# Two stage ends worked tile by tile, and three hand-placed steps moved, in a kernel of two transformer blocks

## What is computed

```python
# first block
h = rmsnorm(x, norm_mix_g); proj = h @ w_in           # pooling mixer and dilated attention on proj
x = x + concatenate([y_pool, y_attn]) @ w_out
h = rmsnorm(x, norm_mlp_g)
x = x + square(relu(h @ w_up)) @ w_down               # hidden width 8192
x = rmsnorm(x, norm_final_g)
# second block; the six mod vectors are silu(c) @ ada_w + ada_b
h = rms(x, norm_g[0]) * (1 + scale_m) + shift_m
proj = h @ w_in_2                                      # differential attention, mLSTM, GLA, S5
o_d = z * sigmoid(z @ s5_glu_w + s5_glu_b)             # z = gelu(S5 scan output), the fourth branch
merged = sum(sigmoid(h @ w_gate[i] + b_gate[i]) * (branch[i] @ w_branch[i]) for i in range(4))
x = x + gate_m * rms(merged @ w_out_2, norm_g[1])
h = rms(x, norm_g[2]) * (1 + scale_f) + shift_f
a, g = split(h @ ffn_w_in)                             # hidden width 5632
x = x + gate_f * rms((silu(a) * g) @ ffn_w_out, norm_g[3])
```

## Time and profile before

| | us |
|---|---|
| median of 3 runs (lowest, highest) | 2698.68 (2697.27, 2699.57) |
| the profiled execution | 2700.24 |
| its span in the profile | 2698.5 |
| PE busy in the span | 2636.2 (98%) |
| DVE busy | 1913.1 (71%) |
| ACT busy | 1251.6 (46%) |
| granted PE clock, mean | 0.995 |

### The profile page before, as it was taken

The page is one execution under the profiler, slowest core; times in us unless marked ns, Lnnn a source line. Parts: engine busy times, 40 slices in busy tenths (PEclk is TensorE's granted clock), DMA queues, the critical chain, the costliest instruction groups (busy, mean ns, idle before and its releaser), DMA issues.

```text
span 2698.5 us, 36266 instructions
## 1 busy us (share of the span) xinstructions
PE 2636.2 (98%) x13230; PEld 2216.3 (82%) x13230; DVE 1913.1 (71%) x2300; ACT 1251.6 (46%) x1515; POOL 280.9 (10%) x322
## 2 busy tenths in 40 slices
PE   8999999999999998999999999999999999999997
PEld 8898888888888886998977777788788888888886
DVE  6676677788778778765676888787755555555686
ACT  5445554444444445455455444444454444444443
POOL 0031041324132000061000000000000000000000
PEclk9999999999999999999999999999999999999999
DMA  9655777888788885856554665688556666666784
GB/s 338 209 162 196 235 261 251 281 275 266 250 282 274 272 271 172 278 165 216 165 164 156 229 217 185 205 306 293 197 184 191 190 191 190 191 188 193 263 292 154
DMA packets 289328, 607.03 MB, mean 225 GB/s; under 512 B 19472, under 2 KB 20688, under 8 KB 287296
## 3 DMA queue, kind: packets, MB, share of 16 engines
q1 hardware_dynamic: 284896, 579.41, 65.3%
q0 software_dynamic: 4320, 26.13, 2.6%
HBM read 594.17 MB, written 11.29 MB: 224 GB/s over the span
## 4 chain that ended last, share of the span: by engine, by line
PE 86%; DVE 6%; DMA 3%; ACT 3%; issue 2%; POOL 0%; SPq 0%; DVEq 0%; ACTq 0%; POOLq 0%
PE ps L577 84%; DVE w_lo L1845 2%; DMA w_raw<-in_w_in 2%; ACT w_hi L1224 1%; DVE arena L1840 1%; PE ps L682 1%; DMA w_raw<-in_w_up 1%; PE ps L709 0%; DMA w_raw<-in_w_gate 0%; DVE x L1855 0%; ACT arena L1482 0%; DMA w_raw<-in_w_down 0%; DVE arena L2174 0%; PE ps L693 0%; PE ps L672 0%
## 5 line engine op out<-in xcount | busy, mean ns | idle before, releaser
L1224 ACT ACTIVATE w_hi<-w_raw 128x1024 fp32r<-128x1024 f32 x900 | 950.6, 1058 | 1356.2 <-PE ps L577 1265.8
L1845 DVE TENSOR_TENSOR w_lo<-w_raw,w_hi 128x1024 fp32r<-128x1024 f32 x812 | 1016.0, 1254 | 653.5 <-ACT w_hi L1224 650.3
L577 PE MATMUL ps<-w_hi,hop_hi_part 128*128 128x512 f32 x2144 | 846.9, 395 | 12.2 <-DVE w_lo L1845 3.1
L577 PE MATMUL ps<-w_hi,hop_lo_part 128*128 128x512 f32 x2144 | 836.7, 390 | 0.0
L577 PE MATMUL ps<-w_lo,hop_hi_part 128*128 128x512 f32 x2144 | 836.3, 390 | 0.0
L577 PEld LDWEIGHTS ps<-w_hi,hop_hi_part 128*128 128x128 f32 x2144 | 403.6, 188 | 109.5 <-issue 15.6
L577 PEld LDWEIGHTS ps<-w_hi,hop_lo_part 128*128 128x128 f32 x2144 | 403.5, 188 | 85.2
L577 PEld LDWEIGHTS ps<-w_lo,hop_hi_part 128*128 128x128 f32 x2144 | 404.0, 188 | 81.1
L577 PE MATMUL ps<-w_hi,hid_hi_part 128*128 128x512 f32 x992 | 389.0, 392 | 5.7 <-DVE x L1855 2.1
L577 PE MATMUL ps<-w_hi,hid_lo_part 128*128 128x512 f32 x992 | 386.3, 389 | 0.0
L577 PE MATMUL ps<-w_lo,hid_hi_part 128*128 128x512 f32 x992 | 386.0, 389 | 0.0
(11 more groups left out here) (308 smaller groups left out, 1525.3 us busy)
## 6 DMA issues: line engine op xcount, KB each, us to landing
arena<-in_ada_w SPq DMA_DIRECT2D x256, 384.0 KB, 4.8
w_raw<-in_ffn_w_in SPq DMA_DIRECT2D x176, 512.0 KB, 3.5
w_raw<-in_w_in SPq DMA_DIRECT2D x152, 512.0 KB, 3.7
w_raw<-in_w_up SPq DMA_DIRECT2D x128, 512.0 KB, 3.9
w_raw<-in_w_down SPq DMA_DIRECT2D x128, 512.0 KB, 4.6
w_raw<-in_w_gate SPq DMA_DIRECT2D x128, 512.0 KB, 4.1
w_raw<-in_ffn_w_out SPq DMA_DIRECT2D x88, 512.0 KB, 3.6
w_raw<-in_w_out SPq DMA_DIRECT2D x64, 512.0 KB, 4.8
```

What stands on the lines that cost most here:

```text
L577: return nc.tensor.matmul(o, w, r, start=start, stop=stop, skip_group_check=True)
L1224: return nc.scalar.activation(o, i, ACT.Copy, scale=scale)
L1845: V.tensor_tensor(w_lo[:, j % LEAD, :, 0:cols], w_raw[:, j % RAW, :, 0:cols], w_hi[:, j % LEAD, :, 0:cols].bitcast(F32), ALU.subtract).the ...
```

## The change

It has four parts. (1) At the end of the MLP, PE waits for each set only where it first writes it, and for the modulation only ahead of the transposes. DVE gives half of the evictions of transposed rows to ACT (banks 1 and 3: `act_turned_half`), each of which waits for the one before it, and DVE and ACT do their steps in another order: the second tile's adds come after the first row has been scaled. (2) The eight `s5_product` steps of PE run two units after their task rather than one, and DVE's `s5_output` one unit later. (3) In the fourth gate the GLU product, the sigmoid, the multiplication and the hi and lo parts come one unit sooner. (4) At the end of the FFN the last four units run tile first, as in the MLP (`tiled_down`); adds, squares, variance, results and output DMAs are done for t = 0 first; the modulation steps are packed closer and end four units sooner, with the copy of the gain and so POOL's two DMAs; DVE waits for `wide` only after the splits of its last loop; ACT loads the inverse-root table ahead of its last four splits. The core of the diff (renamed semaphores left out):

```diff
-ADA_LAST = [22 * g + k + k // 4 for g in range(2) for k in range(KT)]
+ADA_LAST = [20 * g + k + k // 8 for g in range(2) for k in range(KT)]
...
-        for n in range(2):
-            pe.wait_ge(drained[n], H + 5)
-        pe.wait_ge(sem["mod_ready"], G_IN2)
...
+        def tiled_down(R, j0, H, hi, lo, before_last=None):
+            for t in range(TT):
+                for q in range(STAGGER):
+                    n, k = 2 + q // UB, q % UB
+                    if t == 0:
+                        if k == 0:
+                            pe.wait_ge(drained[n % 2], H + 1)
+                        pe.wait_ge(sem["lo_ready"], R * 8 + (j0 + q + 1))
+                    elif q == 3 and before_last:
+                        before_last()
+                    m = token_half(j0 + q, n % 2, t, hi, lo, UK * k, k == 0, k == UB - 1)
...
-                if g == slot[12] + 1:
+                if g == slot[12] + 2:
                     s5_product(t, 0)
-                if g == slot[15] + 1:
+                if g == slot[15] + 2:
                     s5_product(t, 1)
...
-            if u == 3:
+            if u == 2:
                 pe.wait_ge(sem["s_z"], 1)
...
-            if u in (20, 42):
+            if u in (18, 38):
...
-            if u == 45:
+            if u == 41:
                 pe.wait_ge(sem["gain_ready"], 2)
                 turn_gain(4)
...
-        down(R, 48, H + 6, 0, 0, base + FFN_SUPER)
+        for n in range(2):
+            token_chunk(R, 48 + UB * n, H + 6, n, hid_hi[:, 0], hid_lo[:, 0], UB)
+        tiled_down(R, 52, H + 7, hid_hi[:, 0], hid_lo[:, 0])
...
+        def act_turned_half(n, t, b, gain, shift):
+            act.wait_ge(sem["x_turned"], TURNED[n] + STAGGER * t + b + 1)
+            act.wait_ge(sem["xT_ready"], TURNED[n] + STAGGER * t + b)
+            for k in range(2 * b, 2 * b + 2):
+                m = nc.scalar.activation(T(XT + k)[:, t * P:(t + 1) * P], PS[4 + b][:, (k % 2) * P:(k % 2 + 1) * P], ACT.Identity,
+                                         scale=gain[:, k:k + 1], bias=mod[:, shift * KT + k:shift * KT + k + 1])
...
+        inverse_root(tok_guess[:, TT * SUM_MID:TT * SUM_MID + 1], tok_var[:, TT * SUM_MID:TT * SUM_MID + 1])
         for j in range(UA - LEAD):
             split(R + 6, j + LEAD)
...
+        for j in range(UA - LEAD):
+            split(R, j + LEAD)
+            down_ends(R, j, 0, 0, ACC_TOK)
...
+        final_part(2, 0)
+        final_part(3, 0)
+        dve.wait_ge(sem["tok_sums"], 7)
+        row_variance(cols[0], SUM_FFN, 0, 4).then_inc(sem["tok_var"], 1)
+        row_inverse(8, cols[0])
+        result(0, 0)
+        result(0, 1)
+        final_part(2, 1)
+        final_part(3, 1)
+        result(0, 2)
+        dve.wait_ge(sem["tok_sums"], 8)
+        row_variance(cols[1], SUM_FFN, 1, 4).then_inc(sem["tok_var"], 1)
+        result(0, 3)
+        row_inverse(9, cols[1])
         for c in range(4):
+            result(1, c)
```

More of the change, by code:

```diff
@@ L1815, in _, with final_square @@
                 hidden_hi(0, m + 2)
-            if j == 46:
+            if j == 42:
                 act.wait_ge(sem["gain_turned"], 2)
                 copy(gain_rows[64:64 + KT, :], PS[4][64:64 + KT, 0:P]).then_inc(sem["gain_rows"], 1)
+        inverse_root(tok_guess[:, TT * SUM_MID:TT * SUM_MID + 1], tok_var[:, TT * SUM_MID:TT * SUM_MID + 1])
         for j in range(UA - LEAD):
             split(R + 6, j + LEAD)
-        for c in range(4):
-            act.wait_ge(drained[c % 2], R_END_H - 2 + c // 2 + 2)
-            m = token_square(SUM_FFN, c, ACC_TOK, (24, 28, 56, 60)[c])
-        m.then_inc(sem["tok_sums"], 1)
-        token_guess(8, SUM_FFN)
+        for c in range(2):
+            act.wait_ge(drained[c], R_END_H)
+            token_square(SUM_FFN, c, ACC_TOK, (24, 28)[c])
+        def final_square(n, t, spare):
+            act.wait_ge(sem["half_added"], 4 + 2 * t + n - 2 + 1)
+            return nc.scalar.activation(span(spare, 0, COLS), ACC_TOK[:, t, part(n)], ACT.Square,
+                                        accum_out=sums[:, SUM_FFN, t, n:n + 1])
+        for t in range(TT):
+            final_square(2, t, 56 + 4 * t)
+            final_square(3, t, 58 + 4 * t).then_inc(sem["tok_sums"], 1)
+            row_guess(8 + t, TT * SUM_FFN + t)
     @block.vector
@@ L2567, in last_steps @@
                 s5_output(3)
-            if u == 4:
+            if u == 3:
                 dve.wait_ge(sem["s_glu"], 1)
@@ L2742, in _ @@
         R = R + 6
-        dve.wait_ge(sem["wide_in"], 48)
-        for j in range(UA):
-            if j < UA - LEAD:
-                split(R, j + LEAD)
-            down_ends(R, j, 0, 0, ACC_TOK)
-            if j % UB == UB - 1:
-                n = j // UB
-                dve.wait_ge(drained[n % 2], R_END_H - 2 + n // 2 + 2)
-                for t in range(TT):
-                    m = V.tensor_tensor(LAST_TOK[:, t, part(n)], ACC_TOK[:, t, part(n)], wide[:, part(n)], ALU.mult)
-        then(m)
@@ L2754, in _, with final_gain, final_part @@
-        token_variance(8, SUM_FFN, sem["tok_sums"], 7)
-        token_inverse(8, SUM_FFN)
+        for j in range(UA - LEAD):
+            split(R, j + LEAD)
+            down_ends(R, j, 0, 0, ACC_TOK)
+        def final_gain(n, t):
+            return V.tensor_tensor(LAST_TOK[:, t, part(n)], ACC_TOK[:, t, part(n)], wide[:, part(n)], ALU.mult)
+        def final_part(n, t):
+            k = 2 * t + n - 2
+            if t == 0:
+                dve.wait_ge(sem["half_done"], 3 + n - 1)
+            else:
+                dve.wait_ge(sem["unit_done"], R * 8 + LEAD + UB * (n - 1))
+            V.tensor_tensor(ACC_TOK[:, t, part(n)], SETS[n % 2][t][:], ACC_TOK[:, t, part(n)], ALU.add).then_inc(sem["half_added"], 1)
+            dve.wait_ge(sem["half_added"], 4 + k + 1)
+            then(final_gain(n, t))
@@ new lines, in result @@
+        def result(t, c):
+            stt(LAST_TOK[:, t, part(c)], LAST_TOK[:, t, part(c)], inverse(SUM_FFN, t), x_tok[:, t, part(c)],
+                ALU.mult, ALU.add).then_inc(sem["res_ready"], 1)
+        dve.wait_ge(sem["wide_in"], 48)
+        for n in range(2):
+            dve.wait_ge(drained[n], R_END_H)
+            for t in range(TT):
+                then(final_gain(n, t))
+        cols = [TT * SUM_FFN + t for t in range(TT)]
+        final_part(2, 0)
+        final_part(3, 0)
+        dve.wait_ge(sem["tok_sums"], 7)
@@ L2756, in _ @@
+        row_variance(cols[0], SUM_FFN, 0, 4).then_inc(sem["tok_var"], 1)
[9 more added lines that the diff above has]
+        row_inverse(9, cols[1])
         for c in range(4):
-            for t in range(TT):
-                stt(LAST_TOK[:, t, part(c)], LAST_TOK[:, t, part(c)], inverse(SUM_FFN, t), x_tok[:, t, part(c)],
-                    ALU.mult, ALU.add).then_inc(sem["res_ready"], 1)
+            result(1, c)
```

102 lines of the change are left out of this document (51 added, 51 removed).

## The result

| | before | after |
|---|---|---|
| median, us (runs) | 2698.43 (5) | 2683.43 (5) |
| ratio, 95% interval | | 0.9949, 0.9935 to 0.9963 |
| the profiled execution | 2700.24 | 2682.60 |
| its span | 2698.5 | 2680.7 |

The time fell by 15.0 us; 14.4 was forecast, and 2683.43 lies 0.9 under the predicted 2684.3. The page's busy times hardly moved against the earlier trace rows: the gain is idle time of PE that went, and a shorter stretch behind its last matmul.

The account below looks back on a forecast made before the run. PE, busy 98% of the span, was taken to set the time, so only its idle time and the stretch behind it could shrink: -3.5 - 6.6 - 0.7 - 3.6 = -14.4, giving a 2684.3 us median, range 2681.5 to 2689.5.

Parts of the forecast that it names:

- Passage: From the MLP to the in-projection: removed wait, earlier transposes and evictions shared with ACT give -3.5 us, ends -2.0 to -4.2.
- S5: In the gates: running the products one unit later removes five PE waits, -6.6 us, ends -4.5 and -6.8.
- with 0.16 for each: Gates: each of the five waits costs 0.16 us beyond its shown idle time, raising 5.8 to 6.6.
- Fourth branch: Fourth gate: a 1.0 us wait for gelu replaces 1.7 lost on the lo part; -0.7 us, ends -1.5 and +0.5.
- FFN's end: Last FFN units and the stretch behind: PE ends 1.1 us earlier, -3.6 us in all, ends -2.5 and -4.5.
- DVE, not PE, is what sets this end: End of the FFN: DVE's queue sets the finish, reaching the last part 1.3 us after PE is done.
- With the copy four units sooner, it is off the path: End of the FFN: wait behind the splits and copy 10.9 us sooner take the `wide` broadcast off the path.
- B: Rival, gates: half of the 6.6 us won on S5 waits returns as waits for w_lo, 2687.6 us; chance 0.12.
- C: Rival, MLP to in-projection: nothing is won, as evictions wait for the other engine and splits come later; 2687.8 us; chance 0.10.
- D: Rival, whole kernel: the parts don't do what they say, under 5.4 us in all; chance 0.04.
- E: Rival, last FFN stage: packed modulation steps starve it of DMA, 337 GB/s needed against 347 at most; 2706 us; chance 0.04.
- The base: Whole kernel: the profiled execution's 2700.24 us lies 1.56 above the median, so 2685.8 becomes 2684.3.

Follow-up runs that it names:

- part 3 alone: Only the fourth branch's move one unit sooner, applied to the kernel before; median 2696.27 us, ratio 0.9997.
- part 4 alone: Only the tile-first end of the FFN with the earlier gain and moved wait, applied to the kernel before; median 2692.27 us, ratio 0.9983.

## Why the prediction was right

Its sum was made of four terms that were each right in mechanism, and nearly right in size. A fifth was missing: the +0.42 of the output passage, which it took to be left alone.

**Passage, -3.5 forecast.** -4.23 against the profile of before, -3.99 alone. The steps held: the first wait gone, the first transposes at 1043.85 (forecast 1047.6, less the 3.7 by which this run was ahead) behind a wait of 1.13 (1.1 forecast), pair of evictions on ACT 0.79 (0.75 forecast), by ACT's timeline of after:

```profile
1045.84 0.79 ACT L1513 ACTIVATE arena<-ps,mod,gains 128x128 f32<-128x128 f32 x2
```

`rest_rows` started 4.0 sooner (3.8 forecast; 1060.90 against 1068.57, less 3.7). I had 3.8 for the case that the lower clock goes and 2.9 for the case that it stays; the true question was whether before had it at all. Both without it, the gain is 3.17. Of the 1.06 above that (4.23), 0.87 is a fall of the clock that hit the old passage in two of four profiled runs, and 0.2 the wait at 1030.77. So -3.5 lies between what a run with and a run without the fall gives, and which of them it would be was luck. The Trainium skill's rule that I weighed there ("TensorE: Matmul & The Clock Gate", Part 1: The HAM clock gate) fits as far as it goes: it has the throttled state as the one that activity releases, and here idle time of PE was ahead of each fall. No run here shows which idle time brings one on.

**S5, -6.6 forecast.** -5.97. The five waits, 5.81 in all, went, and nothing came back. The step that was mis-sized is "with 0.16 for each". By single matmuls the five were worth 1.45, 1.14, 0.97, 1.11 and 1.29. In the first and the third the product lost the interruption that it had shared, 0.2 each; put those back and the five come to 6.4, so a wait costs some 0.11 beyond the idle time shown. Of the 0.6 by which I was high, 0.2 is that and 0.4 the interruptions that I had not counted.

**Fourth branch, -0.7 forecast.** -0.42 in after, -0.73 alone. The new wait was forecast as 1.0 and was 1.14 or 0.86, depending on the run: ACT's split ahead of gelu started after 1.94 or after 1.66 of idle time. It was 1.14 in three runs and 0.86 in two, one of them part 3 alone and one with everything but ACT's evictions, so it isn't part 2 that makes it. What does stays open.

**FFN's end, -3.6 forecast.** -3.85 (1.09 + 2.76), part 4 alone -3.92. PE's part was forecast as 1.1 and was 1.09 against this profile, but that is luck: the old wait was 0 to 2.5 by the landing of a DMA. "DVE, not PE, is what sets this end" is shown: DVE's last addition started some 1.3 us behind PE, as laid out, and taking products out of its way shortened the end by 0.4 and then 0.75 with PE's end unmoved. "With the copy four units sooner, it is off the path" gave the credit to two edits; the moved wait is enough without the other.

**The rivals.** B and C fell with the four single parts, and D with them: each part did what it says. E had no ground: windows of the last stage moved 359 GB/s at a share of 0.99, more than the 347 that I had taken as the most. A margin worked out from the densest window of a kernel that never asked for more was a bound on the demand, not on the supply.

**The base.** The forecast for the median was made by taking off 1.56 from the profiled run. The medians of before came out at 2698.4 beside after, and at 2697.1, 2696.9, 2699.4 and 2695.5 beside the other kernels. The 0.9 us by which the forecast missed is within that.

## What to carry over

Before a wait is priced from one trace, ask whether its releaser is an engine in lockstep or a DMA: of the first kind most waits here repeated to 0.02 us (the first S5 wait, 1.61 to 1.91, and the one for gelu, 0.86 or 1.14, did not), the second varied by 2.5. When an edit moves both a wait and the work that ends it, test them apart; here the cheap one, moving the wait behind what doesn't need it, was enough, and the packed steps added nothing to it. When a helper gets a new wait, look at every place that calls it: here it cost 0.42 in a passage that the change wasn't meant to touch. And where an engine's queue sets the end, count its work from the last moment at which it was idle: a step helps only if it goes into idle time ahead of that moment, as one product in two did.

## What the hardware showed that I had not expected

The lower clock is partly chance: with the same code and idle times ahead of the fall alike to 0.02 us but for one (0.45 at 1030.77 in before alone), the old passage had a window at 0.50 in two of four profiled runs and none in the two others. A fall costs 0.9 to 1.6 us. Where it comes in every run, in the output passage, keeping it off for one window sped up the transposes from 1.94 to 1.09 and won 0.35, because DVE's evictions set the pace there. The broadcast of the gain from HBM took 6.3 us from issue to landing in one run and 8.1 in another, and PE's wait followed it, from nothing to 2.53 us.
